# SSM mixing in jobs of four heads, filler pieces copied out plain, modulation chunks turned once: a two-layer hybrid backbone on one core

## The reference

```python
# modulation: six vectors of D for each of two conditions, per layer
m = jnp.dot(jax.nn.silu(cond), w) + b            # w is (D, 6 D)

# SSM, one chunk of 128 tokens, heads of a group share B and C
seg = cum_t[..., :, None] - cum_t[..., None, :]
lmat = jnp.where(lower_tri, jnp.exp(jnp.where(lower_tri, seg, 0.0)), 0.0)
cb = jnp.einsum('bcigs,bcjgs->bcgij', cc, bc)
y = jnp.einsum('bcgij,bcghij,bcjghp->bcighp', cb, lmat, xdt)              # within a chunk ("intra")
y = y + jnp.einsum('bcigs,bcghps,bcigh->bcighp', cc, s_prev, jnp.exp(cum)) # from the state ("inter")
y = y + xc * d_skip[..., None]
# gates
g = y * jax.nn.silu(z)                            # SSM, before a group norm
out = sigmoid(gate_logits) * branch               # of each branch, then summed
```

## Time and profile before

| | us |
|---|---|
| median of 3 runs | 3037.94 (3037.47 to 3043.08) |
| the profiled execution | 3034.88, span 3033.6 |
| TensorE busy | 2679.8 (88%) |
| VectorE, ScalarE, POOL busy | 1464.4, 1356.3, 789.1 |

### The profile page before, as it was taken

One profiled execution on the slowest core, in us unless ns is written; L12 is line 12 of the kernel. 1 busy time (PEld: TensorE's weight loads), 2 busy tenths in 40 slices (PEclk: granted clock), 3 DMA queues, 4 the chain that ended last, 5 costly groups with the idle time before them and its releaser, 6 DMA issues. The chain is left out here.

```text
span 3033.6 us, 35314 instructions
## 1 busy us (share of the span) xinstructions
PE 2679.8 (88%) x13423; PEld 2186.5 (72%) x13423; DVE 1464.4 (48%) x1673; ACT 1356.3 (45%) x1713; POOL 789.1 (26%) x356
## 2 busy tenths in 40 slices
PE   4977899999898699998677898888599999999997
PEld 2765678977777588877565677666578888888886
DVE  2353612341332322301443434343378888888887
ACT  2462322331462333322441333435267777677765
POOL 0321244233213344433321553625200000000000
PEclk9978999999999799999787899989789999999998
DMA  6246333223112233322145332423279999999997
GB/s 200 84 127 192 98 90 94 61 69 90 56 42 70 70 97 97 97 84 70 56 125 181 103 110 79 146 63 105 92 271 358 360 354 332 348 369 351 339 337 280
DMA packets 234603, 496.54 MB, mean 164 GB/s; under 512 B 14896, under 2 KB 111440, under 8 KB 234320
## 3 DMA queue, kind: packets, MB, share of 16 engines
q1 hardware_dynamic: 234232, 494.39, 48.1%
q10 hardware_dynamic: 216, 0.07, 0.0%
HBM read 493.37 MB, written 1.05 MB: 163 GB/s over the span
## 5 line engine op out<-in xcount | busy, mean ns | idle before, releaser
L291 POOL TENSOR_TENSOR unit_lo<-raw_units,unit_hi 128x1024 fp32r<-128x1024 f32 x248 | 596.6, 2427 | 1162.9 <-ACT unit_hi L283 1162.9
L2301 DVE TENSOR_TENSOR moe_unit_lo<-moe_raw,moe_unit_hi 128x2048 fp32r<-128x2048 f32 (+1 forms) x283 | 611.9, 2174 | 106.3 <-ACT moe_unit_hi L2295 104.9
L2295 ACT ACTIVATE moe_unit_hi<-moe_raw 128x2048 fp32r<-128x2048 f32 (+1 forms) x283 | 514.8, 1822 | 229.1 <-PE bank L312 221.7
L283 ACT ACTIVATE unit_hi<-raw_units 128x1024 fp32r<-128x1024 f32 (+1 forms) x250 | 247.4, 1039 | 558.7 <-PE bank L312 457.3
L310 PE MATMUL bank<-unit_hi,hT_hi 128*128 128x256 f32 (+1 forms) x1168 | 422.9, 362 | 33.2 <-PEq L1200 13.3
L311 PE MATMUL bank<-unit_lo,hT_hi 128*128 128x256 f32 (+1 forms) x1168 | 402.6, 345 | 0.0
L312 PE MATMUL bank<-unit_hi,hT_lo 128*128 128x256 f32 (+1 forms) x1168 | 401.8, 344 | 0.0
L310 PE MATMUL bank<-moe_unit_hi,xe_T_hi 128*128 128x512 f32 (+1 forms) x768 | 290.4, 378 | 1.1 <-DVE xe_T_lo L2332 1.1
L310 PEld LDWEIGHTS bank<-unit_hi,hT_hi 128*128 128x128 f32 x1168 | 229.5, 197 | 84.8 <-issue 52.2
L311 PE MATMUL bank<-moe_unit_lo,xe_T_hi 128*128 128x512 f32 (+1 forms) x768 | 286.8, 373 | 0.0
L312 PE MATMUL bank<-moe_unit_hi,xe_T_lo 128*128 128x512 f32 (+1 forms) x768 | 286.3, 373 | 0.0
(11 more groups left out here) (381 smaller groups left out, 4325.5 us busy)
## 6 DMA issues: line engine op xcount, KB each, us to landing
moe_raw<-in_moe_w SPq DMA_DIRECT2D x224, 1024.0 KB, 7.4
raw_units<-in_w_in SPq DMA_DIRECT2D x160, 512.0 KB, 3.7
moe_raw<-in_moe_w SPq DMA_DIRECT2D x64, 768.0 KB, 4.3
ada_unit<-in_ada_w SPq DMA_DIRECT2D x40, 1024.0 KB, 5.4
raw_units<-in_ffn_w SPq DMA_DIRECT2D x66, 512.0 KB, 3.7
raw_units<-in_w_branch SPq DMA_DIRECT2D x48, 512.0 KB, 3.5
ada_first<-in_ada_w SPq DMA_DIRECT2D x8, 1024.0 KB, 12.2
raw_units<-in_w_out SPq DMA_DIRECT2D x16, 512.0 KB, 3.6
```

Of the source, the lines that this page charges most:

```text
L283: act.activation(half_of(view(whi, g), half), half_of(view(raw, g), half), ACT.Copy).then_inc(hi_ready, 1)
L291: eng.tensor_tensor(lo, whole, hi.bitcast(F32), ALU.subtract).then_inc(lo_ready, 1)
L2295: act.activation(moe_hi[:, at_unit % RING, 0:n], moe_raw[:, at_unit % SLOTS, 0:n], ACT.Copy).then_inc(hi_m, 1)
L2301: dve.tensor_tensor(moe_lo[:, at_unit % SLOTS, 0:n], moe_raw[:, at_unit % SLOTS, 0:n], moe_hi[:, at_unit % RING, 0:n].bitcast(F32), ALU.su ...
```

## The change

Six things, all between the projections and the gates:

1. `ssm_mix` works in half-jobs of 4 heads (`halves`, 16 and 8 of them) over four buffers of `seg` and `side`; a half-job's intra products come two slots later, behind that slot's modulation unit and filler piece.
2. The filler of `ssm_mix` has a weight for each slot: 0 for six slots in `ssm_project`, 6 for one slot at the head of `ssm_mix`, 1 for each other slot (34 and 26 of them). The attention filler gets a slot of weight 0 in `att_project`.
3. Filler pieces of z and of the attention gate are copied out with Copy; Silu is taken in `ssm_gate`, Sigmoid in `merge(2)`, both in place in `xres` by activations of 512 columns.
4. Modulation units are spread over the slots but the last two, and the four units of a chunk accumulate into one row block (the window of `cond` that is multiplied shifts by two columns a unit), which is copied and turned once, by two matmuls of 8 columns.
5. `ret_project` turns the q heads inside the last product, over four banks.
6. `ssm_project` turns over banks 4 and 5 and no longer over 5, 6 and 7.

```diff
-            def __init__(self, l, name, tiles, func, slots):
+            def __init__(self, l, name, tiles, func, weights):
...
-                self.edges = [self.total * i // slots for i in range(slots + 1)]
+                at_slot = np.cumsum([0] + list(weights))
+                self.edges = [int(round(self.total * x / at_slot[-1])) for x in at_slot]
...
-        def ada_rows(pe, out, buf):
+        def ada_rows(pe, out, buf, row=0, first=True, last_unit=True):
...
-                last = pe.matmul(out[32 * j:32 * j + 32, :], cond[:, k, :], buf[:, k, :], start=k < 4, stop=k >= 4)
+                last = pe.matmul(out[32 * j:32 * j + 32, :], cond[:, k, 6 - 2 * row:38 - 2 * row], buf[:, k, :],
+                                 start=first and k < 4, stop=last_unit and k >= 4)
...
-                        if i >= 3:
-                            pe.wait_ge(turned_out, i - 2)
+                        if i >= 2:
+                            pe.wait_ge(turned_out, i - 1)
...
+        Z_TAIL, Z_HEAD = [0, 0], [6, 6]
+
+        def ssm_slots(tiles):
+            return 2 * SG * len(tiles) + 2 + 2 * SG * NT
...
-            seg = at("segments", [P, 2, HG, P], F32, outT_at + 16384)
-            side = at("dt_side", [P, 2, HG, P], F32, outT_at + 24576)
+            seg = at("segments", [P, 4, 4, P], F32, outT_at + 16384)
+            side = at("dt_side", [P, 4, 4, P], F32, outT_at + 24576)
...
+            halves = 2 * len(jobs)
+            slots = ssm_slots(tiles)
+            ada_at = [len(ada_units) * i // (slots - 2) for i in range(slots - 1)]
...
                 def _(sp):
+                    fill.load(sp, 6)
                     for i in range(2):
                         load_ada(sp, i)
                     for slot in range(slots):
-                        fill.load(sp, slot)
-                        if 2 <= slot + 2 < len(ada_units):
-                            load_ada(sp, slot + 2)
...
+                        fill.load(sp, 7 + slot)
+                        for i in ada_in_slot(slot):
+                            if i + 2 < len(ada_units):
+                                load_ada(sp, i + 2)
...
                 def _(act):
...
+                    fill.act(act, 6)
+                    for m in range(slots):
+                        if m < halves:
+                            tile, g = jobs[m // 2]
+                            act.wait_ge(seg_sum, m + 1)
+                            if m >= 4:
+                                act.wait_ge(intra, m - 3)
+                            act.activation(seg[:, m % 4, :, :], ps[2 + m % 2][:, :].rearrange("p (h i) -> p h i", h=4),
+                                           ACT.Copy).then_inc(backward, 1)
...
+                            act.wait_ge(seg_out, m + 1)
+                            act.activation(seg[:, m % 4, :, :], seg[:, m % 4, :, :], ACT.Exp).then_inc(seg_exp, 1)
+                        for i in ada_in_slot(m):
+                            if i % ADA_U == ADA_U - 1:
+                                act.wait_ge(ada_used, i + 1)
...
+                                act.activation(ada_row[:, :], ps[4][:, 0:256], ACT.Copy).then_inc(ada_out, 1)
+                        fill.act(act, 7 + m)
...
+                    for m in range(halves):
+                        if m + 1 < halves:
+                            segments(m + 1)
+                        mix(m)
+                        if m % 2 and m >= 3:
+                            add_intra(m // 2 - 1)
...
+                    fill.pe(pe, 6)
+                    pe.wait_ge(lhs_ready, 1)
+                    pe.wait_ge(coef_ready, 1)
+                    for m in range(halves + 2):
+                        if m < halves:
...
+                            if m >= 2:
+                                pe.wait_ge(seg_out, m - 1)
...
+                        modulation(m)
+                        fill.pe(pe, 7 + m)
+                        if m >= 2:
+                            n, half = divmod(m - 2, 2)
...
+                            pe.wait_ge(mixed, m - 1)
```

In `ssm_gate`, ScalarE's queue:

```diff
-                    split_hi(act, a0 + 1)
+                    for g in range(SG):
+                        for tile in tiles:
+                            z = xres[:, tile if l == 0 else tile - 2, g * 512:(g + 1) * 512]
+                            act.activation(z, z, ACT.Silu).then_inc(silu_out, 1)
+                        if g == 0:
+                            split_hi(act, a0 + 1)
```

In `merge(2)`, ScalarE's queue:

```diff
-                        for g in range(a0 + 2, b0 + 1):
-                            split_hi(act, g)
+                        for b in range(2):
+                            for tile in tiles:
+                                sg = xres[:, tile if l == 0 else tile - 2, b * 512:(b + 1) * 512]
+                                act.activation(sg, sg, ACT.Sigmoid).then_inc(gate_out, 1)
+                            for g in range(a0 + 2, b0 + 1)[2 * b:2 * b + 2]:
+                                split_hi(act, g)
```

In `ret_project`, TensorE's queue:

```diff
-                        project(pe, a0 + 2 * n, banks[n], blocks[n])
-                    pe.wait_ge(out, done[3])
+                        for u in range(2):
+                            project_half(pe, a0 + 2 * n, u, banks[n], blocks[n])
+                            if n == 3 and u == 0:
+                                pe.wait_ge(out, done[2])
+                                for i in range(RH):
+                                    turn(i)
+                    for i in range(RH, 2 * RH):
+                        turn(i)
```

More of the change, by code:

```diff
@@ L654, in _ @@
                     loads(sp, f"ssm{l}")
+                    for slot in range(6):
+                        fill.load(sp, slot)
                 @block.gpsimd
@@ L658, in _ @@
                     splits_lo(pool, f"ssm{l}", 2)
+                    for slot in range(6):
+                        fill.lo(pool, slot)
                 @block.scalar
@@ L680, in _ @@
                             act.activation(u_of(i), acc[:, m, :], ACT.Silu).then_inc(u_ready, 1)
+                        if n == 2:
+                            for slot in range(6):
+                                fill.act(act, slot)
                         act.wait_ge(u_ready, 4 * n + 4)
@@ L893, in _ @@
                 @block.gpsimd
                 def _(pool):
[L895 to L901 removed]
+                    fill.lo(pool, 6)
@@ new lines, in _ @@
+                    for slot in range(slots):
+                        fill.lo(pool, 7 + slot)
+                        if slot < len(jobs):
+                            tile, g = jobs[slot]
+                            pool.wait_ge(coef_ready, 1)
+                            pool.tensor_tensor(by_head(y[:, tile, g * 512:(g + 1) * 512]), by_head(xtok[:, tile, g * 512:(g + 1) * 512]),
+                                               wide(coef[:, HG * slot:HG * slot + HG]), ALU.mult).then_inc(skipped, 1)
@@ L1391, in _, with turn @@
                 def _(pe):
+                    def turn(i):
+                        src, h, tiles = (qtok, i, q_tiles) if i < RH else (ktok, i - RH, ALL_TILES)
+                        if i >= 4:
+                            pe.wait_ge(turned_out, i - 3)
+                        for j, tile in enumerate(tiles):
+                            last = pe.transpose(ps[i % 4][:, j * P:(j + 1) * P], src[:, tile, h * DK:(h + 1) * DK], ident)
+                        last.then_inc(turned, 1)
                     for n in range(4):
@@ L1418, in ret_mix @@
             steps = [(s, d) for s in range(NT) for d in range(2)]
[L1419 removed]
+            fill = Filler(l, "rf", tiles, ACT.Silu, [1] * (n + 1 + len(steps)))
             def w_of(kind, d):
@@ L1677, in att_mix @@
             jobs = [(tile, kv) for tile in tiles for kv in range(KVH)]
-            slots = sum(1 + (2 if tile < 2 else NT) for tile, kv in jobs)
-            fill = Filler(l, "gf", tiles, ACT.Sigmoid, slots)
+            slots = range(1, 1 + att_slots(tiles))
             def sc(i, job):
@@ L1690, in _ @@
                 def _(sp):
-                    for slot in range(slots):
+                    for slot in slots:
                         fill.load(sp, slot)
```

242 lines of the change are left out of this document (107 added, 135 removed).

## The result

The changed kernel takes 2997.5 us (median; 2995.0 to 2999.7) against 3037.7 for the kernel before, run beside it: a ratio of 0.986, with a 95% interval of 0.985 to 0.988. The gain is 40 us where 55.5 were forecast. Its profiled execution took 2999.7 us, its span is 2998.4, so 35.2 less than the span of before.

A forecast was written before the change was run, and what follows sets the result against it. TensorE, busy 88% of the span, bounds the kernel, with idle time and low clock in SSM mixing. Mixing -51, attention -8, gate +2.9, projections -1.4 and +2 take 3037.9 us to 2982.4; range 2950 to 3018.

The forecast's parts named there:

- the prediction's own signs: SSM mixing: windows near 162, 110 us; segment waits near nothing; two weight stalls of 7 to 9 us a layer.
- Part 2: SSM mixing, half-jobs over four buffers: layer 0's 13.0 us wait for VectorE's segments goes; 4 and 3 us put back.
- Part 4: SSM mixing, modulation units spread over slots: stalls for weights move but stay, 17 us in layer 0, 12.5 in layer 1.
- Part 3: SSM mixing, each chunk's modulation rows turned once: 7.7 and 5.2 us less TensorE time, at 0.43 us a turn.
- Part 1: Head of SSM mixing, filler ahead of the jobs: jobs start at 174.1 to 174.5 (layer 0) and 1570.5 (layer 1).
- Part 6: Plain copies, Silu and Sigmoid later: attention -4 us in each layer, gates +2.4 (layer 1) and +0.5 (layer 0).
- Part 7: Projections: retention turns inside gain 0.8 and 0.6 us; SSM projection over two banks costs 1 us a layer.
- The sum: Whole kernel: -51 (SSM mixing) - 8 + 2.9 - 1.4 + 2 = -55.5 us, giving 2982.4.
- A: SSM mixing's losses stay, the job chain being as long as before, and only work moves: 3015 us, chance 0.21.
- B: SSM mixing's stalls for weights go, the loaded units outlasting the boundary: -29.5 and some 8 us, 2945; chance 0.12.
- C: Slower: in SSM mixing unit boundaries feed themselves through split, loads and half-job; 12 us more each, 3054; chance 0.07.
- D: No change: ScalarE's table loads stay, since a plain copy might bring its own; 3030 us, chance 0.02.

The follow-up runs named there:

- run 5: Changed kernel with whole jobs of eight heads over two buffers and VectorE's order of before, all other parts kept: 3003.8 us, ratio 0.989.
- run 1: Changed kernel with VectorE's add into y issued ahead of the next half's minimum and mask multiplies: 2981.8 us, ratio 0.981.
- run 4: Changed kernel with no filler at the head of SSM mixing (weight zero in both layers): 3016.8 us, ratio 0.992.
- run 6: Changed kernel with the add issued early and SyncE's modulation loads first, raw-unit load three slots later: 2965.1 us, ratio 0.976.
- run 10: Changed kernel with SyncE's order alone changed (modulation loads first, raw-unit load three slots later), add still late: 2994.2 us, ratio 0.984.
- run 12: Kernel before with SyncE's order alone changed (modulation load first, raw-unit load three slots later): 2998.4 us, ratio 0.986.
- run 2: Changed kernel with each modulation unit's rows copied and turned separately, accumulation off: 3020.3 us, ratio 0.994.
- run 11: Changed kernel with early add, SyncE's modulation loads first and raw-unit load three slots later, and no filler at the head: 2966.8 us, ratio 0.976.
- run 3: Changed kernel with Silu and Sigmoid again at the filler pieces, plain copies undone: 3008.2 us, ratio 0.989.
- run 7: Changed kernel with SSM projection turns over three banks and retention turns behind the last copies, as before: 2999.5 us, ratio 0.988.

## Why the prediction was right, and where it was not

The sign and the rough size held. But the stage totals came near for a reason that is in part luck: two errors of some 21 us run against each other in them. Two of the prediction's own signs failed too: there were not two stalls of 7 to 9 us for weights in each layer, and a wait stood first that it does not name.

**Part 2, the 13.0 us taken as gone: wrong.** The wait for the segments did go (0.6 left), but I priced VectorE's work in a slot (2.4 us against 3.2 for TensorE) and not the order in its queue. Layer 1's 5.4 us for the segments, which also went, the working does not name. The add stands behind a chain that begins with ScalarE's copy, and that brought 12.8 and 9.1 us. I put the half-jobs at 9 us (13.0 less 4) in layer 0; run 5 gives a gain of 5.8 there, and a loss of 0.4 in layer 1. Run 1 is the proof that it was order and not work: the same instructions, 4.1 and 8.8 us less.

**Part 4, stalls of 17 and 12.5 us: wrong in size, right in mechanism.** 2.5 and 6.3 came. The layout had slots of 3.2 us. In run 1 slot 4 begins about where the layout has it (186.3 for 187.3), but slots 4 to 6, in which the first boundary stands, take 12.8 us and not 9.5: there are waits of 0.9 us for the copy of a chunk and 1.1 for the add, behind a VectorE multiply of 2.73 us beside POOL's split, and then intra products at 1.94 us for 1.00. So TensorE comes to the missing unit at 199.9 (layout 196.8), and the data is there at 204.8 (layout 204.3). The loads were timed rightly, and TensorE's arrival was not. In the changed kernel the wait for the add makes the slots longer still (4.5 us each up to the last half-job, 4.1 in run 1). That is only a part of the miss: without it run 1 still shows about half of the forecast (8.9 and 7.0 for 17 and 12.5). Runs 1 and 4 show the stalls return once slots shorten or the boundaries move (8.9, 13.9), and runs 6, 10 and 12 that they come from SyncE's place behind POOL's split, as the earlier trace rows showed. The prediction says of that queue that it "stays as it is" and stops there. Run 12 was to be read out of the earlier trace rows.

**Part 3, turns at 0.43: too low as work.** 7.7 and 5.2 us were forecast, and run 2 gives 17.2 and 2.9. The price was one pair of starts at the upper clock; run 2 has 0.67 us of busy time a turn in layer 0 and 0.58 in layer 1. The group's mean over the stage of before would have been the better price, 13.8 us for 24 turns:
```profile
L446 PE MATMUL bank<-constants,ada_row 128*128 128x2 f32 x96 | 13.8, 248 | 0.0
```
The rest of the miss is no price of a turn: in layer 0 a lower clock on all other matmuls adds 4.5 us, in layer 1 a wait hides half of the turns.

**Part 1, the head.** First half-job in layer 0 at 174.08, forecast 174.1 to 174.5; in layer 1 11.1 us after the stage began, forecast 10.7 (by the rows the three pieces would start at 1564.8 and not at 1564.3, so 11.2). But in layer 1 it was not the pieces that set this start: TensorE had finished them and idled 4.5 us for VectorE. The prediction had the cause, a VectorE operation stretched beside POOL's split, and put its 2 to 4 us "under the head". They were not. VectorE's preparation in the changed kernel beside the head's split, then in run 4 with no split there:
```profile
1541.01 4.79 POOL L291 TENSOR_TENSOR unit_lo<-raw_units,unit_hi 128x1024 fp32r<-128x1024 f32 x2 [21.02 <-ACT unit_hi L283]
1542.14 1.40 DVE L992 TENSOR_SCALAR cum_lhs<-cum_part,constants 128x256 fp32r<-128x256 f32 x1
1543.46 2.48 DVE L993 TENSOR_SCALAR cum_row<-cum_part,constants 128x256 f32<-128x256 f32 x1
```
```profile
1552.51 0.41 DVE L992 TENSOR_SCALAR cum_lhs<-cum_part,constants 128x256 fp32r<-128x256 f32 x1
1552.84 0.41 DVE L993 TENSOR_SCALAR cum_row<-cum_part,constants 128x256 f32<-128x256 f32 x1
```
That is 3.1 us, and run 4's first half-job stands 8.0 us after its stage began. The head's value was put at 3.3 and 2.4 us (half-pieces taken from the slots less the later start); run 4 gives 14.4 and 6.4, mostly through the weights, and run 11 -4.8 and 8.6 without that cause. So the head's worth seems to be where it puts the splits, which the working had only for SyncE; no run moved a split alone.

**Part 6, plain copies.** Attention -4.0 and -1.7 (forecast -4 and -4), the gates of layer 1 and layer 0 +2.4 and -0.6 (+2.4 and +0.5). In layer 1's attention the wait that was to go, 2.9 us for att_probs_T, is still 2.8, and a longer one, 4.9 us for the exponentials, stands in both kernels; the earlier trace rows don't show it. The table loads in attention of layer 0 were 16 in the kernel before, and one is left:
```profile
L1761 ACT ACT_TABLE_LOAD x1 | 1.3, 1283 | 0.3 <-PEq L1657 0.3
```
By the Trainium skill's page ScalarE: Activation LUTs, section What ACT_TABLE_LOAD costs, with its further drain of 1.38 us for each switch, the gain would have been twice the 4 us. The stage shows 4.0, and the trace shows no drain beside the 1.28. One of the loads of before, with the activation right behind it:
```profile
827.85 1.28 ACT L1705 ACT_TABLE_LOAD   x1
829.14 0.47 ACT L1705 ACTIVATE att_probs<-bank,small 128x256 f32<-128x256 f32 x1
```
In SSM mixing I had nothing for the copies; run 3 gives 5.7 and 3.2.

**Part 7.** Two banks cost 1.5 and 1.7 where I had 1 (the first lies within what layer 0 scatters, by run 7). The retention turns gained 1.0 and 0.6 at equal clock (0.8 and 0.6 forecast). Not foreseen: rounding moved the retention filler's edges, 2.7 us in layer 1.

**The sum.** Mixing was put at -51 and gave -39.8. The new wait (21.9 us) and the stalls that did not happen (29.5 less 8.8, so 20.7) nearly cancel. Of the size of the 11 that are missing are x_weighted in layer 0 (5.7 where I had 0) and skip_coef in layer 1 (4.5 where I had 0); that they are the 11 is argued, not shown. The parts measured one by one in layer 0 (5.8, 17.2, 14.4, 5.7) sum to 43 against 24.1: each one undone lets another wait show, so they are not terms of a sum. The other stages were put at -4.5 and gave +4.6 in the profiles: 4.2 from retention mixing, 3.5 more from the retention projections (clock, by run 7) and 1.9 from the retention gates (the 1.5 of layer 0 with the clock at 0.94 for 1.00), 2.4 more from the SSM projections, 2.3 from attention in layer 1. Against these, the routing and the last stage read 4.3 less; the change has no code there, and run 12, old but for one queue, reads 3.1 less too.

**The rivals.** A (losses stay, 3015) is in part what happened: run 5 shows that the half-jobs as given bought 5.8 and -0.4 us, since a new wait took the place of the old, though not by the longer chain that A names. The turns and the head, with what hangs on them, gained more than A had. B (stalls go, 2945) had the stalls nearly right; it did not have the wait for the add, and so not the time. C (slower) did not occur: no boundary fed the next. D (no change) fell.

What stays open is what the two waits for VectorE are worth, 4.5 us for x_weighted in layer 0's steps and 4.5 for skip_coef at layer 1's start. Both stand beside a split. In layer 0 it is POOL's from 280.39 to 285.52, and two VectorE operations that take 0.69 us elsewhere took 2.75 and 2.82 there:
```profile
283.24 2.82 DVE L1038 TENSOR_TENSOR ssm_state<-ssm_state,ssm_decay 128x512 f32<-128x512 f32 x1
...
287.44 2.08 PE L1122 MATMUL bank<-x_weighted,B_tok 128*128 128x512 f32 x2 [4.49 <-DVE x_weighted L1025]
```
No run moved these splits and left the rest as it was.

## What to carry to other kernels

Before a gain is booked for a wait that goes, write out the queue of the engine that frees the buffer, instruction by instruction: the wait that comes next is often an instruction standing behind a chain it doesn't need. A DMA queue is such a queue as well: a load that must wait belongs behind the loads that needn't, and in the kernel before that one move was worth as much as all parts of this change (in the changed one, alone, it gave 3 us). Two waits that cover each other must be removed together (4.1 and 0.9 us alone, 17.0 together).

## What the runs showed of the hardware

The granted clock of a stage whose own code is unchanged differs from one profiled execution to the next. Whether the stages ahead of it set that, or it differs between executions of one kernel too, was not tested. Retention mixing of layer 1, with the same instructions in both, in run 6 and in run 11:
```profile
1770.30:1827.70 57.40, 49.76 (x304) 45.48 (x304) 29.82 (x48) 14.43 (x21) 19.24 (x8) 0.94 0.24 74
```
```profile
1772.70:1827.10 54.40, 46.77 (x304) 42.81 (x305) 31.20 (x48) 14.43 (x21) 19.26 (x8) 1.00 0.26 78
```
3.0 us of busy time for 0.06 of clock, so a part of 1 or 2 us can only be read between executions that had the same clock in its stage. In run 7 the mixing stage of layer 1, unchanged, was busy for 94.8 us at 0.78, against 87.3 at 0.84 in the changed kernel; 5.8 us less idle time hid most of that.

VectorE operations that run beside one of POOL's splits take longer: 2.48 us for 0.41 at the start of layer 1, 2.75 and 2.82 for 0.69 in layer 0's steps. That POOL is the cause rests on these pairs and on run 4, where the split was not beside them.
